# Experts: one run of twelve transpositions per block, each split over two halves of the array's rows

## The reference, cut to what matters

```python
def hierarchical_moe(x, w_rg, b_rg, w_re, b_re, w1, w3, w2):
    ...
    eid = (g_sel[:, None] * EXPERTS_PER_GROUP + top_i).reshape(-1)   # 2 of 32 experts per token
    order = jnp.argsort(eid)
    ...
    xs = xf[tok_s]                                                    # rows, gathered by expert
    h = jax.nn.silu(lax.ragged_dot(xs, w1, sizes)) * lax.ragged_dot(xs, w3, sizes)
    o = lax.ragged_dot(h, w2, sizes) * gate_s[:, None].astype(x.dtype)
    y = jnp.zeros_like(xf).at[tok_s].add(o)                           # added back to their tokens
```

## Time and profile before

| | |
|---|---|
| median of 3 runs | 5428.47 us (5426.96 to 5434.37) |
| the profiled execution | 5415.57 us, its span 5413.6 us |
| busy share of the span | PE 93%, DVE 71%, ACT 54%, POOL 24% |
| mean granted TensorE clock | 0.965 |

### The profile page before, as it was taken

The page is one execution under the profiler, slowest core; times in us unless marked ns, Lnnn a source line. Parts: engine busy times, 40 slices in busy tenths (PEclk is TensorE's granted clock), DMA queues, the critical chain, the costliest instruction groups (busy, mean ns, idle before and its releaser), DMA issues. The chain is left out here.

```text
span 5413.6 us, 109648 instructions
## 1 busy us (share of the span) xinstructions
PE 5046.7 (93%) x36030; PEld 4371.9 (81%) x36031; DVE 3841.7 (71%) x6531; ACT 2904.1 (54%) x4721; POOL 1285.4 (24%) x1184
## 2 busy tenths in 40 slices
PE   8999999999989997969999958998999997999994
PEld 6989798988989996858888847888888886888883
DVE  6778887687766667776886847876555556866887
ACT  3343444344378885555665634442788213645765
POOL 2111020000011110044554532210100003543655
PEclk9999999999999998979999979999999997999997
DMA  6776765355499996578998856654655436987997
GB/s 213 217 205 210 205 211 173 119 168 129 133 313 318 315 305 195 181 282 298 311 349 260 309 163 219 217 184 134 214 162 162 135 127 229 333 261 232 369 327 253
DMA packets 755209, 1237.10 MB, mean 229 GB/s; under 512 B 111838, under 2 KB 407277, under 8 KB 754828
## 3 DMA queue, kind: packets, MB, share of 16 engines
q1 hardware_dynamic: 630108, 877.59, 49.8%
q0 software_dynamic: 75312, 286.28, 17.0%
q10 hardware_dynamic: 49408, 68.17, 3.8%
HBM read 917.08 MB, written 333.67 MB: 231 GB/s over the span
## 5 line engine op out<-in xcount | busy, mean ns | idle before, releaser
L622 PE MATMUL qa_ps_out<-qa_x_hi,qa_w_hi 128*128 128x512 f32 x1344 | 529.3, 394 | 22.8 <-DVE qa_w_lo L784 12.9
L622 PE MATMUL qa_ps_out<-qa_x_lo,qa_w_hi 128*128 128x512 f32 x1344 | 525.0, 391 | 0.0
L622 PE MATMUL qa_ps_out<-qa_x_hi,qa_w_lo 128*128 128x512 f32 x1344 | 524.9, 391 | 0.0
L668 ACT ACTIVATE qa_w_hi<-qa_w_whole 128x1024 fp32r<-128x1024 f32 x180 | 191.2, 1062 | 429.5 <-PE qa_ps_out L622 223.9
L622 PE MATMUL qa_ps_out<-qa_w_hi,qa_x_hi 128*128 128x256 f32 x1344 | 381.4, 284 | 0.0
L622 PE MATMUL qa_ps_out<-qa_w_hi,qa_x_lo 128*128 128x256 f32 x1344 | 380.4, 283 | 0.0
L622 PE MATMUL qa_ps_out<-qa_w_lo,qa_x_hi 128*128 128x256 f32 x1344 | 380.3, 283 | 0.0
L1336 ACT ACTIVATE da_prob<-da_minus_s,da_rows 128x256 f32<-128x256 f32 (+1 forms) x768 | 317.7, 464 | 41.9 <-DVE da_rows L1304 41.9
L1304 DVE CUSTOM_DVE_ANT_0 da_minus_s<-da_ps_s,da_bias 128x256 f32<-128x256 f32 (+1 forms) x768 | 259.8, 375 | 90.5 <-PE da_ps_s L1235 81.3
L622 PEld LDWEIGHTS qa_ps_out<-qa_x_hi,qa_w_hi 128*128 128x128 f32 x1344 | 253.5, 189 | 80.7 <-DVE qa_w_lo L784 17.5
L2915 DVE CUSTOM_DVE_ANT_0 ga_minus_s<-ga_ps_s,ga_bias 128x512 f32<-128x512 f32 (+1 forms) x256 | 185.4, 725 | 175.4 <-PE ga_ps_s L2837 163.9
(11 more groups left out here) (526 smaller groups left out, 15365.4 us busy)
## 6 DMA issues: line engine op xcount, KB each, us to landing
a_ex_w_raw<-w SPq DMA_DIRECT2D x128, 1024.0 KB, 10.2
b_ex_w_raw<-w SPq DMA_DIRECT2D x128, 1024.0 KB, 10.2
qa_w_raw<-w_qkv_a SPq DMA_DIRECT2D x144, 512.0 KB, 4.8
a_ex_w_raw<-w POOLq DMA_DIRECT2D x66, 1024.0 KB, 8.5
b_ex_w_raw<-w POOLq DMA_DIRECT2D x66, 1024.0 KB, 8.3
da_q_cross<-qT SPq DMA_DIRECT2D x48, 1024.0 KB, 7.7
da_k_parts<-kT SPq DMA_DIRECT2D x48, 1024.0 KB, 10.2
a_in_o<-o SPq DMA_DIRECT2D x16, 1584.0 KB, 8.1
```

The lines of the kernel that those rows point to most:

```text
L622: done = pe.matmul(out, stationary, moving, start=(k == 0 and i == 0), stop=(k == KH - 1 and i == 2))
L668: act.activation(w_hi[:, p % W_RING], src, ACT.Copy).then_inc(w_hi_done, 1)
```

## The change

1. TensorE's body becomes `up(b)`, `down(b - 1)`, `turn_h(b)`, `turn_x(b + 2)`: the twelve transpositions follow each other at the end of the body, and those of the rows are for the block two ahead. The first two blocks are written out before the loop.
2. Each 128 x 128 transposition becomes two: 64 rows (tokens 0 to 63 on the upper half of the array's rows, 64 to 127 on the lower), 128 stationary columns, 64 moving columns of the identity. Each half of the tokens goes to its own PSUM bank. Ahead of each group of transpositions TensorE increments a semaphore that nobody waits for (`x_turning`, `h_turning`).
3. ACT and DVE take the 1024 transposed columns of a block in one call each instead of two, and put the two banks' halves in their places (`by_half`).
4. POOL gathers the rows ahead of its two low parts instead of behind them.

```diff
-        ps_x = ps("ps_x", [P, 2, 4, P])
+        ps_x = ps("ps_x", [P, 2, KC, HD])
-        ps_h = ps("ps_h", [P, FC, P])
+        ps_h_banks = ps("ps_h", [P, 2, HALF])
+        ps_h = ps_h_banks[:, :, 0:FC * HD].rearrange("p r (k n) -> p r k n", n=HD)
+        def by_half(turned):
+            return turned.rearrange("p k (r n) -> p r k n", r=2)
...
                 def turn_x(b):
                     pe.wait_ge(x_loaded, 16 * b + 16)
                     for h in range(2):
                         if not first(b):
                             pe.wait_ge(x_lo, 2 * b + h - 1)
+                        pe.sem_inc(x_turning, 1)
                         for k in range(4):
-                            done = pe.transpose(ps_x[:, h, k, :], x_row[:, bass.ts(4 * h + k, P)], ident[:])
+                            for r in range(2):
+                                toks = bass.ts(r, HD)
+                                done = pe.transpose(ps_x[:, r, 4 * h + k, :], x_row[toks, bass.ts(4 * h + k, P)],
+                                                    ident[toks, toks], tile_position=(HD * r, 0))
                         done.then_inc(x_turned, 1)
...
                 def turn_h(b):
+                    pe.sem_inc(h_turning, 1)
                     for k in range(FC):
-                        done = pe.transpose(ps_h[:, k, :], gate[:, bass.ts(k, P)], ident[:])
+                        for r in range(2):
+                            toks = bass.ts(r, HD)
+                            done = pe.transpose(ps_h[:, r, k, :], gate[toks, bass.ts(k, P)], ident[toks, toks],
+                                                tile_position=(HD * r, 0))
...
                 turn_x(0)
                 up(0, Block(pe, 0).count)
                 turn_x(1)
                 turn_h(0)
+                second = Block(pe, 1)
+                up(1, second.count)
+                turn_x(2)
+                down(0, second.before)
+                turn_h(1)
+                turn_x(3)
                 def body(b, at):
                     up(b, at.count)
-                    turn_x(b + 1)
                     down(b - 1, at.before)
                     turn_h(b)
-                over_blocks(pe, body)
+                    turn_x(b + 2)
+                over_blocks(pe, body, 2)
...
ACT          def x_parts(b):
-                    for h in range(2):
-                        act.wait_ge(x_turned, 2 * b + h + 3)
-                        act.activation(xT_hi[:, 4 * h:4 * h + 4, :], ps_x[:, h], ACT.Copy).then_inc(x_hi, 1)
+                    act.wait_ge(x_turned, 2 * b + 4)
+                    act.activation(by_half(xT_hi[:]), ps_x[:], ACT.Copy).then_inc(x_hi, 2)
DVE          def x_parts(b):
-                    (two calls of 512 columns)
+                    dve.tensor_tensor(by_half(xT_lo[:]), ps_x[:], by_half(xT_hi[:].bitcast(F32)), ALU.subtract
+                                      ).then_inc(x_lo, 2)
...
POOL         def rest(b, at):
+                    gather_x(b + 2)
                     with pool.If(at.next_new > 0):
                         split_w13(pool, b + 1, ...)
-                    gather_x(b + 2)
                     with pool.If(at.new > 0):
                         next_w2(b, at.count)
```

More of the change, by code:

```diff
@@ L2321, in experts @@
         x_loaded = sem("x_loaded")
+        x_turning = sem("x_turning")
+        h_turning = sem("h_turning")
         x_turned = sem("x_turned")
@@ L2514, in x_parts @@
                 def x_parts(b):
-                    for h in range(2):
-                        act.wait_ge(x_turned, 2 * b + h + 3)
-                        act.wait_ge(w13_used, W13_PIECES * b + W13_PIECES)
-                        act.activation(xT_hi[:, 4 * h:4 * h + 4, :], ps_x[:, h], ACT.Copy).then_inc(x_hi, 1)
+                    act.wait_ge(x_turned, 2 * b + 4)
+                    act.wait_ge(w13_used, W13_PIECES * b + W13_PIECES)
+                    act.activation(by_half(xT_hi[:]), ps_x[:], ACT.Copy).then_inc(x_hi, 2)
                 def split_w2(b, n):
@@ L2532, in h_parts @@
                     act.wait_ge(w2_used, W2_PIECES * b + W2_PIECES)
-                    act.activation(hT_hi[:], ps_h[:], ACT.Copy).then_inc(h_hi, 1)
+                    act.activation(by_half(hT_hi[:]), ps_h, ACT.Copy).then_inc(h_hi, 1)
                 def block_of(b, at):
@@ L2568, in x_parts @@
                 def x_parts(b):
[L2569 to L2573, removed]
+                    dve.wait_ge(x_hi, 2 * b + 2)
+                    dve.tensor_tensor(by_half(xT_lo[:]), ps_x[:], by_half(xT_hi[:].bitcast(F32)), ALU.subtract
+                                      ).then_inc(x_lo, 2)
                 def outputs(b):
@@ L2587, in h_parts @@
                     dve.wait_ge(h_hi, b + 1)
-                    dve.tensor_tensor(hT_lo[:], ps_h[:], hT_hi[:].bitcast(F32), ALU.subtract).then_inc(h_lo, 1)
+                    dve.tensor_tensor(by_half(hT_lo[:]), ps_h, by_half(hT_hi[:].bitcast(F32)), ALU.subtract
+                                      ).then_inc(h_lo, 1)
                 def split_w2(b, n):
```

## The result

The changed kernel takes **5578.77 us** (median of 5 runs, 5576.68 to 5583.64), against 5428.47: 2.8% slower, ratio 1.0276 with a 95% interval of 1.0262 to 1.0290. The forecast was 5540, with a range of 5450 to 5600. Its profiled execution has a span of 5575.5 us.

A forecast was written before the change was run, and what follows sets the result against it. The prediction took TensorE's own stream to bound the expert loops. Switch 30, late gathers 62, half clock 24, DVE's lateness gone -6 and extra first-block work 2 sum to 112 us, giving 5540 us, range 5450 to 5600.

The forecast's parts named there:

- I take a pair at 0.11 us: the load is as long as its columns.: Split transpositions on TensorE: twelve pairs cost 1.33 us a block, as now, so no gain; bounds 0.06 and 0.22 a pair.
- 0.33 a round trip: TensorE's switch between whole and split matmuls and back: 0.33 us for each of 91 blocks, 30 us more.
- The bound with increments that drain: Upper bound of the switch's price: semaphore increments also drain TensorE, twice 0.15 us more inside the run, 57 us in all.
- Part 1: One run of twelve transpositions on TensorE instead of two runs: nothing by itself, each transposition costs the same.
- Part 3: Rows gathered two blocks ahead: TensorE waits for the late gather in 23 blocks, 2.7 us each, 62 us; bounds 39 and 106.
- behind all the others: In queue q0 the gather gets through only after two w2 loads and the add, 3.15 MB with it; TensorE stands 1.7 us.
- The 6 us that I had counted back: DVE's present lateness in long runs of new experts, idle time of TensorE, goes away: -6 us.
- The clock: After 14 of 23 stalls TensorE runs 3.4 us at half clock, losing 1.7 each: 24 us, bounds 0 and 39.
- A: Rival: the gather is in time, no stall, only the switch between whole and split matmuls costs; 5458 us, chance 0.12.
- D: Rival: halved load makes TensorE's stream 25 us shorter, faster only with fewer than about six stalls; 5403 us, chance 0.07.
- B: Rival: the halves load one after the other, 1.66 us more a block, hardly a stall left; 5583 us, chance 0.14.
- C: Rival: loading 64 rows takes half the time, -0.27 us a block, but stalls for the gather remain; 5489 us, chance 0.12.

The follow-up runs named there:

- the first cure: The changed kernel with POOL's gather for block b + 2 moved ahead of the add: 5511.21 us, ratio 1.0153.

## Why the prediction was right or wrong

**The sign and the size** were right, 5579 for 5540, but through errors that partly cancel, so that the size is in part luck: the sum lacks a loss of 90 us and also a gain of 55.

**"I take a pair at 0.11 us: the load is as long as its columns."** Wrong: 0.06, the lower bound. I chose by the number of stationary columns. The 0.060 of the earlier trace rows, 128 rows by 64 columns, and the 0.06 here, 64 rows by 128, say that half of the array loads in half the time whichever way it is halved. Both runs also have half the moving columns, but these don't make it: whole loads with 64 moving columns start (7.03 - 0.40) / 31 = 0.21 apart at half clock, as the next run's with 128 do, and that is twice 0.11:

```profile
4500.01 7.03 PE L1947 MATMUL b_rt_ps_tokens<-b_rt_token_at,b_rt_at_offset 128*128 128x64 f32 x32 [9.13 <-ACT b_rt_token_at L1970]
4508.01 7.09 PE L1954 MATMUL b_rt_ps_gates<-b_rt_gate_at,b_rt_at_offset 128*128 128x128 f32 x32 [0.97 <-DVE b_rt_gate_at L2101]
```

The rule of the Trainium skill, "TensorE: Matmul & The Clock Gate", section on LDWEIGHTS, by which the number of rows makes no difference, doesn't hold in this trace (its estimate is 0.107 us a pair, and 0.06 was measured). "TensorEngine Tiling (Array Packing)" of the Trainium skill, section on the theoretical speedup, is borne out: a pair costs half.

**"0.33 a round trip."** Right: 0.33 from the split alone. The bound with increments that drain was not met.

**Part 1, "one run instead of two: nothing by itself."** For whole transpositions that is nearly so: 17.65 to 17.75 in two of three of that run's blocks without a stall. The step that failed is that the sum has no term for parts 1 and 2 together. The run now stands at the end of the body, right ahead of the loop's register code, and the split run gives the sequencer too little time to get ahead. That takes a block from 17.43 to 18.36, 0.93 us, with the 0.25 in later blocks 90 us in all. I had costed the moved instructions on TensorE and the queues of POOL, and not the sequencer's own work. With the pairs' gain (91 x 0.6 = 55 us) the two errors leave 35 us too little.

**Part 3, the late gather**: 23 stalls by 2.7 forecast, 24 by 1.8 measured (62 and 44 us), in the short leads and by turns. The leads were as expected (10.0 to 10.4 in all but a few of them), the landings quicker: I had taken the slow end of the earlier trace rows, 11.2 for the add, and the one above landed after 9.3. Where I said why, I was half wrong: "behind all the others" in q0. The count of bytes was right and the cause wasn't: without the w2 loads the gather is as late. The 6 us that I had counted back are there (5.7), and the loops' ends took them again (7.1).

**The clock**: 24 us forecast, 40 measured. I had priced the stall's own length, and there is now a second pause, the gap, behind each: in the block at 4733.74 TensorE stood 2.16 us, ran the eight pairs and stood 1.10 more, and the granted clock over the next 3.4 us was 0.52 (the columns are those of the earlier trace rows):

```profile
4738.20:4741.60 3.40, 3.40 (x8) 2.73 (x9) 3.17 (x5) 0.22 (x1) 0.76 (x1) 0.52 1.05 393
```

**The rivals.** A and D fall with the stalls. B reached the right time, 5583, by a mechanism that isn't there. C had the array right to 0.01 us a block and missed the gap.

With the measured terms the forecast's sum of 112 becomes 112 + 35 - 18 (stalls) + 16 (clock) = 145, against 150.

## What to carry to other kernels

- Work that is moved to the end of a loop's body is moved next to the loop's register code. Ask what covers it: long instructions ahead of it do, many short ones don't, nor does a wait that the sequencer stands in. A gap named after a semaphore that was set long ago, or after nothing, is the sign; look at the sequencer's own rows.
- A switch between whole and split matmuls has a fixed price; gather the split work into one run, and the run must be long enough: here 12 pairs save 0.6 us and pay 0.33.
- Before a transfer is needed earlier, look at what stands ahead of it: both in its queue, and in the program of the engine that issues it. Here the first cure was an order of two lines (68 us).

## What the runs showed of the hardware

- A pair of 64 x 128 loads with 64 moving columns, one on each half of the array's rows, costs 0.06 us; a whole 128 x 128 transposition 0.11. In which order the program lists the halves makes no difference (one run).
- The sequencer's lead over the array looks like a count of instructions, 32 in all three places where it can be read. The wait ahead of the second four of rows is let through (L2424) when the hidden run starts, at 4869.03; in program order 16 loads and 16 matmuls stand between the two. In the kernel before, the word is read 2.7 us ahead of the hidden run, which is 12 products (24 instructions) and the four transpositions' 8. With whole transpositions in the new order it is read at the earliest 0.9 us ahead, 4 products (8) and the twelve transpositions' 24. This is worked out from the order of the programs; no run varied the count by itself.

```profile
L2424 PEldq EVENT_SEMAPHORE  x1: 51/51/51, 4869.1 to 4869.1; - x1
```

- An indirect add of 0.5 MB lands 6 to 11 us behind its issue, 6.1 with no other traffic at the start; in the case above a gather issued 3.7 us behind it landed 2 us after it, with nothing else in the queue.
- In the changed kernel none of the 62 blocks that have the gap alone (1.05 to 1.4 us, once 2.2) was followed by half clock; with 1.8 to 2.2 us in each block 27 of 46 were.
